# Gate and up products of an fp32 feed-forward layer: seven block products per pair of weight units in place of per unit

## What is computed

```python
D_MODEL, SEQ, D_FF = 1024, 256, 2816
x = rms_norm_2(h, g_pre_ffn)                  # 256 x 1024
gate, up = split(x @ w_gate_up, 2, axis=-1)   # w_gate_up: 1024 x 5632
y = (silu(gate) * up) @ w_down                # w_down: 2816 x 1024
h = h + rms_norm_2(y, g_post_ffn)
```

## Time and profile before

| | |
|---|---|
| median of three runs | 1509.06 us (1507.21 to 1509.69) |
| the profiled execution | 1509.1 us |
| its span, first to last instruction | 1507.3 us |
| mean granted TensorE clock | 0.948 |
| TensorE busy over the span | 1258.5 us (83%) |
| VectorE, ScalarE, GpSimd busy | 426.8, 283.0, 49.9 us |
| moved by DMA | 493.24 MB, mean 327 GB/s |

### The profile page before, as it was taken

One profiled execution on the slowest core, in us unless ns is written; L12 is line 12 of the kernel. 1 busy time (PEld: TensorE's weight loads), 2 busy tenths in 40 slices (PEclk: granted clock), 3 DMA queues, 4 the chain that ended last, 5 costly groups with the idle time before them and its releaser, 6 DMA issues.

```text
span 1507.3 us, 32779 instructions
## 1 busy us (share of the span) xinstructions
PE 1258.5 (83%) x14574; PEld 925.6 (61%) x14574; DVE 426.8 (28%) x862; ACT 283.0 (19%) x687; POOL 49.9 (3%) x90
## 2 busy tenths in 40 slices
PE   8999977678777778687776777777899999999998
PEld 5565855556555556565555565565555586888854
DVE  1653222122121121221221211212224213466644
ACT  3433212011121110210120111111212222211100
POOL 4101000000000000000000000000100000000000
PEclk9999999999899997998999899989999999999999
DMA  9529899999999999999999999999963342464420
GB/s 342 191 90 363 365 428 427 429 428 429 429 427 429 428 429 430 427 429 427 429 430 427 429 427 429 430 427 429 404 236 110 112 163 76 139 196 168 167 84 28
DMA packets 78597, 493.24 MB, mean 327 GB/s; under 512 B 4856, under 2 KB 28624, under 8 KB 53856
## 3 DMA queue, kind: packets, MB, share of 16 engines
q1 hardware_dynamic: 76560, 486.69, 78.8%
q0 software_dynamic: 1600, 5.17, 1.2%
q10 hardware_dynamic: 400, 0.86, 0.1%
HBM read 491.65 MB, written 1.05 MB: 327 GB/s over the span
## 4 chain that ended last, share of the span: by engine, by line
DMA 54%; PE 44%; issue 1%; DVE 1%; POOL 1%; SPq 0%; ACT 0%; DVEq 0%; POOLq 0%
DMA ring<-in_w_gate_dram 45%; PE bank L1345 7%; PE bank L1056 6%; PE bank L1157 6%; PE bank L690 5%; DMA ring<-in_w_down_dram 5%; PE bank L1380 4%; PE bank L777 3%; PE bank L714 2%; PE bank L1310 2%; DMA ring<-in_w_up_dram 2%; PE bank L1085 1%; PE bank L671 1%; DMA ring<-in_w_in_dram 1%; PE bank L1071 1%
## 5 line engine op out<-in xcount | busy, mean ns | idle before, releaser
L1056 PE MATMUL bank<-ring,big 128*32 128x128 f32 x8192 | 301.3, 309 | 179.7 <-DMA ring<-in_w_gate_dram 119.5
L1056 PEld LDWEIGHTS bank<-ring,big 128*32 128x32 f32 x8192 | 260.5, 124 | 230.2 <-DMA ring<-in_w_gate_dram 90.6
L1085 PE MATMUL bank<-ring,big 128*32 128x256 f32 x2048 | 130.2, 395 | 46.8 <-DMA ring<-in_w_down_dram 46.1
L2099 DVE TENSOR_TENSOR big<-big,bank 128x128 f32<-128x128 f32 x64 | 24.2, 378 | 470.6 <-PE bank L1056 470.6
L1600 ACT ACTIVATE big<-bank 32x256 f32<-32x256 f32 x128 | 47.9, 374 | 438.1 <-PE bank L1085 436.6
L1085 PEld LDWEIGHTS bank<-ring,big 128*32 128x32 f32 x2048 | 67.1, 112 | 86.2 <-issue 34.2
L2110 DVE COPY big<-bank 32x256 f32<-32x256 f32 x128 | 54.1, 423 | 226.8 <-PE bank L1085 224.9
L1157 PE MATMUL bank<-ring,xT 128*128 128x512 f32 x192 | 85.2, 594 | 0.3 <-ACT xT L1439 0.3
L690 PE MATMUL bank<-ring,xT 128*128 128x512 f32 x192 | 84.0, 593 | 0.0
L1071 PEld LDWEIGHTS bank<-aux,c 128*128 128x128 f32 x512 | 65.5, 201 | 15.0 <-issue 15.0
L1071 PE MATMUL bank<-aux,c 128*128 x512 | 74.3, 290 | 0.0
(11 more groups left out here) (373 smaller groups left out, 1408.2 us busy)
## 6 DMA issues: line engine op xcount, KB each, us to landing
ring<-in_w_gate_dram SPq DMA_DIRECT2D x64, 2048.0 KB, 25.8
ring<-in_w_up_dram SPq DMA_DIRECT2D x64, 2048.0 KB, 27.1
ring<-in_w_down_dram SPq DMA_DIRECT2D x63, 2048.0 KB, 27.1
ring<-in_w_gate_up_dram SPq DMA_DIRECT2D x22, 1024.0 KB, 7.0
ring<-in_w_in_dram SPq DMA_DIRECT2D x14, 1024.0 KB, 17.3
ring<-in_w_down_dram SPq DMA_DIRECT2D x12, 1024.0 KB, 6.9
ring<-in_w_in_dram SPq DMA_DIRECT2D x3, 2048.0 KB, 27.0
ring<-in_w_out_dram SPq DMA_DIRECT2D x2, 2048.0 KB, 18.3
```

Of the source, the lines that this page charges most:

```text
L1056: i = pe.matmul(dst[TOK * j:TOK * (j + 1), 0:P], xg[:, k, TOK * q:TOK * (q + 1)], w[:, k, j * P:(j + 1) * P], start=(k == 0), stop=(k == K ...
L1085: i = pe.matmul(bank[6 + q % 2][TOK * m:TOK * (m + 1), 0:SEQ], hT[:, q % 2, TOK * k:TOK * (k + 1)], w[:, k, SEQ * m:SEQ * (m + 1)], start= ...
```

## The change

`GU_FIRST` becomes 1: one plain unit, with two calls of `hidden` per token tile. The other ten units are taken as five pairs. The column halves of the block scheme are now the two units of a pair, so a block is 512 columns wide (256 gate, 256 up), a block product is four matmuls of 512 columns into a whole bank, and a weight sum covers 2048 elements a partition. There is one home for t1, t2 and t4 in place of two; the sums of the next pair's t1 and t2 wait for P5 of this pair, t4 for P4. TensorE's order becomes P1, P6, first turn of the pair before, P2, second turn, P5, P7, wait for ScalarE's copy of P7 (and for t4), P4, P3. The first slot of a pair is handed back after P4, the second after P3. A turn still has four transposes; each pair has two. The sums signal one by one (`gs_T`), and the buffers for P1, P7, P5 and the joined results exist once. The down products use other banks and homes, in the same order; the turns of the last pair come before P5 and before P7 of the first down unit.

```diff
-GU_FIRST = 2
-GU_SEVEN = N_GU - GU_FIRST
+GU_FIRST = 1
+GU_PAIRS = (N_GU - GU_FIRST) // 2
...
-                         *(("gu_mm", 2 * u + 2) if u < GU_FIRST else ("gs_mm", 7 * (u - GU_FIRST) + 7))))
+                         *(("gu_mm", 2 * u + 2) if u < GU_FIRST else ("gs_mm", 7 * ((u - GU_FIRST) // 2) + 6 + (u - GU_FIRST) % 2))))
...
         def gate_up_parts(i):
 
-            w = post_slot(12 + GU_FIRST + i).rearrange("p (j k w n c) -> p j k w n c", j=2, k=4, w=2, n=2)
-            return ([w[:, j, :, :, n, :] for j in range(2) for n in range(2)],
-                    [gs_T[i % 2][:, 1024 * m:1024 * (m + 1)].rearrange("p (k w c) -> p k w c", k=4, w=2) for m in range(3)])
+            w = [post_slot(12 + GU_FIRST + 2 * i + n).rearrange("p (j k c) -> p j k c", j=2, k=4) for n in range(2)]
+            return [w[n][:, j, :, :] for j in range(2) for n in range(2)], gs_T
 
         def gate_up_bank(i, m):
-            return bank[(4 * (i + 1) + m) % 7][:, 0:SEQ]
-
-        def gate_up_buffers(i):
-
-            b = (xn_flat[:, 0:1536], aux[:, 6144:7680])[i % 2]
-            return ([b[:, SEQ * m:SEQ * (m + 1)] for m in range(3)], b[:, 768:1536].rearrange("p (m w c) -> p m w c", m=3, w=2),
-                    xn_flat[:, 1536 + P * (i % 2):1536 + P * (i % 2 + 1)])
-
-        gs_T = [aux[:, 0:3072], aux[:, 3072:6144]]
+            return bank[(4 * (i + 1) + m) % 7][:, :]
+
+        gs_T = [aux[:, 2048 * m:2048 * (m + 1)].rearrange("p (k c) -> p k c", k=4) for m in range(3)]
+        gs_p1, gs_p7, gs_p5 = (xn_flat[:, 512 * m:512 * (m + 1)] for m in range(3))
+        gs_e11 = [xn_flat[:, 1536 + 256 * n:1536 + 256 * (n + 1)] for n in range(2)]
+        gs_quads = aux[:, 6144:7680].rearrange("p (m w c) -> p m w c", m=3, w=2)
...
-            for j in range(4):
+            for j in range(2 * GU_FIRST):
...
-            for j in range(4):
+            for j in range(2 * GU_FIRST):
                 hidden(j, P, SEQ)
+            def gate_up_turn(i, n):
+
+                rows = (gs_e11[i % 2], gs_quads[:, 1, 0, :]) if n == 0 else (gs_quads[:, 0, 0, :], gs_quads[:, 2, 0, :])
+                pe.wait_ge(*gs_at("gated", i))
+                pe.wait_ge(*at("ff_h", 2 * (GU_FIRST + 2 * i + n)))
+                for c in range(2):
+                    for t in range(TT):
+                        k = pe.transpose(bank[7][:, (2 * c + t) * P:(2 * c + t + 1) * P], rows[t][:, c * P:(c + 1) * P], ident)
                 k.then_inc(S("gs_tp"), 1)
...
                 def block_product(m, left, right, first):
                     for k in range(4):
-                        j = pe.matmul(gate_up_bank(i, m), left[:, k, :], right[:, k, :, :], start=(first and k == 0), stop=(k == 3),
+                        j = pe.matmul(gate_up_bank(i, m), left[:, k, :], right[:, k, :], start=(first and k == 0), stop=(k == 3),
                                       skip_group_check=not first)
                     j.then_inc(S("gs_mm"), 1)
 
-                post_wait(pe, 12 + GU_FIRST + i)
+                post_wait(pe, 12 + GU_FIRST + 2 * i)
                 if i >= 2:
                     pe.wait_ge(*gs_at("join", i - 2))
                 block_product(0, gs_x[0][0], b11, True)
-                pe.wait_ge(*gs_at("sums", i))
+                pe.wait_ge(*gs_at("t2", i))
                 block_product(1, s2, t2, True)
+                if i >= 1:
+                    gate_up_turn(i - 1, 0)
                 pe.wait_ge(*gs_at("p1", i))
                 block_product(0, gs_x[0][1], b21, False)
+                pe.wait_ge(*at("ff_h", 2 * GU_FIRST))
                 if i >= 1:
-                    gate_up_turn(i - 1)
+                    gate_up_turn(i - 1, 1)
+                block_product(3, s1, t1, True)
+                pe.wait_ge(*gs_at("b12", i))
                 block_product(2, s3, b12, True)
-                if i >= 1:
-                    pe.wait_ge(*gs_at("mult11", i - 1))
-                pe.wait_ge(*at("ff_h", 4))
-                block_product(3, s1, t1, True)
                 pe.wait_ge(*gs_at("p7", i))
+                pe.wait_ge(*gs_at("t4", i))
                 block_product(2, gs_x[1][1], t4, False)
-                pe.wait_ge(*gs_at("p5", i))
                 block_product(3, s4, b22, False)
...
-                        pe.wait_ge(*gs_at("join", GU_SEVEN - 2))
+                        pe.wait_ge(*gs_at("join", GU_PAIRS - 2))
                     if (n, name) == (0, "P5"):
-                        gate_up_turn(GU_SEVEN - 1)
+                        gate_up_turn(GU_PAIRS - 1, 0)
+                    if (n, name) == (0, "P7"):
+                        gate_up_turn(GU_PAIRS - 1, 1)
...
+            for i in range(GU_PAIRS):
                 if i >= 1:
                     gate_up_rest(i - 1)
                 act.wait_ge(*at("gs_mm", 7 * i + 1))
-                A(p1, gate_up_bank(i, 0), ACT.Copy).then_inc(S("gs_act"), 1)
+                A(gs_p1, gate_up_bank(i, 0), ACT.Copy).then_inc(S("gs_act"), 1)
+                if i >= 1:
+                    gate_up_turned(i - 1, 0)
                 act.wait_ge(*at("gs_mm", 7 * i + 3))
                 if i >= 2:
-                    act.wait_ge(*at("gs_tp", i - 1))
-                A(e11, gate_up_bank(i, 0)[:, 0:P], ACT.Silu).then_inc(S("gs_act"), 1)
+                    act.wait_ge(*at("gs_tp", 2 * i - 3))
+                A(gs_e11[i % 2], gate_up_bank(i, 0)[:, 0:256], ACT.Silu).then_inc(S("gs_act"), 1)
+                if i >= 1:
+                    gate_up_turned(i - 1, 1)
                 act.wait_ge(*at("gs_mm", 7 * i + 4))
-                A(p7, gate_up_bank(i, 2), ACT.Copy).then_inc(S("gs_act"), 1)
-                if i >= 1:
-                    gate_up_turned(i - 1)
+                A(gs_p5, gate_up_bank(i, 3), ACT.Copy).then_inc(S("gs_act"), 1)
                 act.wait_ge(*at("gs_mm", 7 * i + 5))
-                A(p5, gate_up_bank(i, 3), ACT.Copy).then_inc(S("gs_act"), 1)
-            gate_up_rest(GU_SEVEN - 1)
-            gate_up_turned(GU_SEVEN - 1)
+                A(gs_p7, gate_up_bank(i, 2), ACT.Copy).then_inc(S("gs_act"), 1)
...
                 if part == 0:
-                    post_wait(dve, 12 + GU_FIRST + i)
-                    if i >= 2:
-                        dve.wait_ge(*at("gs_mm", 7 * i - 7))
-                    link(V.tensor_tensor(t1, b12, b11, ALU.subtract))
+                    for n in range(2):
+                        post_wait(dve, 12 + GU_FIRST + 2 * i + n)
+                    if i >= 1:
+                        dve.wait_ge(*at("gs_mm", 7 * (i - 1) + 4))
+                    V.tensor_tensor(t1, b12, b11, ALU.subtract).then_inc(S("gs_T"), 1)
+                    dve.wait_ge(*gs_at("t1", i))
                 elif part == 1:
-                    link(V.tensor_tensor(t2, b22, t1, ALU.subtract))
+                    V.tensor_tensor(t2, b22, t1, ALU.subtract).then_inc(S("gs_T"), 1)
+                    dve.wait_ge(*gs_at("t2", i))
                 elif part == 2:
-                    V.tensor_tensor(b12, b22, b12, ALU.subtract)
+                    V.tensor_tensor(b12, b22, b12, ALU.subtract).then_inc(S("gs_T"), 1)
                 else:
-                    V.tensor_tensor(t4, b21, t2, ALU.subtract).then_inc(S("gs_dve"), 1)
+                    if i >= 1:
+                        dve.wait_ge(*at("gs_mm", 7 * (i - 1) + 6))
+                    V.tensor_tensor(t4, b21, t2, ALU.subtract).then_inc(S("gs_T"), 1)
...
+                if i >= 1:
+                    gate_up_gate(i - 1)
+                dve.wait_ge(*at("gs_mm", 7 * i + 2))
+                dve.wait_ge(*gs_at("p1", i))
+                link(V.tensor_tensor(gs_p1, gs_p1, gate_up_bank(i, 1), ALU.add))
+                if i >= 1:
+                    down_rows(i - 1)
+                dve.wait_ge(*gs_at("silu11", i))
+                V.tensor_tensor(e11, e11, gate_up_bank(i, 0)[:, 256:512], ALU.mult).then_inc(S("gs_dve"), 1)
                 if more:
                     gate_up_sums(i + 1, 0)
+                    gate_up_sums(i + 1, 1)
+                else:
+                    down_sums(0)
+                dve.wait_ge(*gs_at("p7", i))
+                link(V.tensor_tensor(gs_p7, gs_p7, gs_p1, ALU.add))
                 if i >= 1:
-                    gate_up_gate(i - 1)
-                if more:
-                    gate_up_sums(i + 1, 1)
-                dve.wait_ge(*at("gs_mm", 7 * i + 2))
-                dve.wait_ge(*gs_at("p1", i))
-                link(V.tensor_tensor(p1, p1, gate_up_bank(i, 1), ALU.add))
+                    dve.wait_ge(*at("gs_tp", 2 * i))
+                V.tensor_tensor(c22, gs_p7, gs_p5, ALU.add)
                 if more:
                     gate_up_sums(i + 1, 2)
                     gate_up_sums(i + 1, 3)
-                else:
-                    down_sums(0)
-                dve.wait_ge(*gs_at("silu11", i))
-                V.tensor_tensor(e11, e11, gate_up_bank(i, 0)[:, P:2 * P], ALU.mult).then_inc(S("gs_dve"), 1)
-                dve.wait_ge(*gs_at("p7", i))
```

(58 more changed lines are left out.)

5 lines of the change are left out of this document (3 added, 2 removed).

## The result

The changed kernel takes 1513.41 us (median of 10 runs, 1511.43 to 1515.79) against 1508.68 for the kernel before (10 runs, 1506.94 to 1512.46): ratio 1.0029, 95% interval 1.0019 to 1.0039, so slower by some 0.3%. The profiled execution took 1513.1 us, its span is 1511.3, mean granted clock 0.943.

The account below looks back on a forecast made before the run. TensorE's gapless stream after 1291.87 was taken to bound the end one for one. -2.51 + 1.52 + 4.90 = +3.91 us on 1509.06 gave 1513.0 us (+0.26%), range 1508.0 to 1516.0.

Parts of the forecast that it names:

- The work itself: TensorE's plain and block products: one plain unit dropped, wider blocks, one turn more; net -2.51 us.
- The width's 0.7: Block products: doubling the width alone saves 0.7 us over 35 products.
- The start loses cover: Before the second tile's plain products: TensorE waits for ScalarE's copy of that tile, +1.52 us (1.34 to 1.7).
- A wait without cover in every pair: Between P7 and P4: ScalarE's copy of P7 is uncovered, 0.98 us in five pairs, +4.9 us (4.0 to 5.5).
- After the pairs: Down products begin at about 1437.2 instead of 1433.83; after that TensorE's stream is as long as now.
- What stays hidden: Inside the pairs: sums, "gated", turns and unit loads come in time, 9.9 us spare for next sums; no wait.
- The clock: Stretch of pairs: granted clock stays 1.00, no term; rival has it at 0.91, +11.9 us, 1524.9 us, chance 0.04.
- the P7 wait costs nothing: Rival, between fifth and sixth product: the bank's copy is covered, sum -1.0, 1508.1 us; chance 0.15.
- the single home costs time: Rival, at P6: next pair's t1 and t2 come only after "gated", 4.0 us four times, 1529 us; chance 0.03.
- the wide product's cost: Rival, block products: a wide one isn't twice the narrow; at 3.35 each, -2.9 us more, 1510.1 us; chance 0.02.

Follow-up runs that it names:

- the new order in the kernel before: Kernel before (256 columns, two homes, two plain units) with only P5 issued ahead of P7: 1514.72 us, ratio 1.0042.
- the two narrow matmuls: Changed kernel with every 512-column block matmul issued as two of 256 columns, weights loaded for each: one run, 1517.79 us, stretch 210.46 us.
- the turn in the gap: Changed kernel with the second turn of four transposes moved from before P5 to between P7 and P4: one profiled run, stretch 207.99 us.

## Why the prediction was right

1513.0 us was forecast and 1513.41 measured; the stretch was to grow by 3.91 us and grew by 3.81. That the time came within 0.4 us is in part luck: the forecast started from 1509.06, ten runs beside the changed kernel gave 1508.68, and from there it would have said 1512.6. The stretch is the better witness. Step by step:

- *The work itself, -2.51.* With both waits removed the stretch is 2.47 under that of before. The width's 0.7 was measured by itself as 0.69. Right.
- *The start loses cover, +1.52.* Issuing P1 early took 1.51 off. Right. The forecast 1301.62 had the slower first load in it; measured are 1301.69 and 0.10 for that load, less the 0.19 by which the whole stretch is later: 1301.60.
- *A wait without cover in every pair, +4.90.* Measured 0.95 rather than 0.98 a pair, 4.78 by the run that took it away. The mechanism is right, the term 0.12 too large: I charged 0.08 between the copy and the weight load, from a place where VectorE's copy ended last; after ScalarE's copy it is 0.04.
- *After the pairs.* The down products were to begin at about 1437.2 and began at 1437.39, 0.19 of it from ahead. But the stream behind that was not "as long as now": 64.44 us to the last piece in place of 64.00, since the added turn lies in the first down unit. The sum counts that turn once, with the work of the pairs, so it stands; only the place was wrong.
- *What stays hidden.* No wait on VectorE or on a transfer. 2048 elements take 2.29 us, as extended from shorter rows; "gated" ends 2.75 into the second pair (1335.72 + 0.96 - 1333.93), forecast 2.8. The single home was no matter even 3.4 us later.
- *The clock.* The granted clock stayed 1.00, with idles of 0.69 us in 26 and also with those of 1.18 where the copy was doubled. This is that kernel's row, again with the columns of the earlier trace rows; the clock is the 1.00 near its end. The Trainium skill (page "TensorE: Matmul & The Clock Gate", section "A second HAM failure mode: psum-queue depth-cycling") reports for a bf16 kernel that short idles between groups of matmuls make the clock oscillate. These fp32 runs do not show it: the clock is 1.00 in every stretch above.

```profile
1320.00:1440.00 120.00, 114.12 (x288) 51.05 (x287) 68.89 (x68) 21.23 (x36) 0.00 (x0) 1.00 0.44 151
```

- *Rivals.* That the P7 wait costs nothing is refuted by five idles; that the single home costs time, by the run with P7 first and by the new order in the kernel before; the wide product's cost by the rows at 3.43.

What is not settled: the medians differ by 4.73 us and the stretches by 3.81. The interval of the ratio, +2.9 to +5.9 us, holds both, so the runs do not show that the rest needs a cause.

## What to carry to other kernels

When two products share a bank and the first must be copied out before the second may start, the products between them are what hides the copy; changing their order (here P5 went first, whose sum t1 is there before P7's b12) puts copy and hand-off on the path, once per round. Widening a matmul from 256 to 512 columns saved almost nothing here (a product took 3.454 us in two halves and 3.433 whole), so judge such a change by the waits that it makes and by the work that it drops. Work that is dropped may have been cover: look for what lay beside it, and move up something that needs only the inputs already there.

## What the runs showed of the hardware

The stretch does not begin at the same time in each execution: between 1290.48 and 1296.06 us in eleven profiles, although all edits lie behind that point. That is more than the 3.81 us of the change, while the stretch itself gave the same length to 0.01 us (203.49 and 203.50 in two executions of one kernel). For an edit behind such a start, the stretch tells from one profile what the total needs many runs for.

The spread is older than the expert loop. From the start of the loop's last piece to the start of the stretch all eleven took 215.29 or 215.30 us, and the loop itself, from its first product to that piece, 919.1 to 919.9. But its first product started anywhere from 155.84 to 160.98, and that goes with TensorE's granted clock. In the four latest (159.2 and more) the clock was 0.94 from 30 to 60 us and 0.96 or 0.97 from 100 to 155; in the four next (157.5 to 157.7) 1.00 and 0.97; in the three earliest (up to 156.3) 1.00 in both. Here are the latest, with the two narrow matmuls, and the earliest but one, with the turn in the gap; columns as in the earlier trace rows.

```profile
30.00:60.00 30.00, 28.69 (x88) 17.07 (x89) 12.65 (x15) 13.92 (x25) 6.57 (x4) 0.94 0.80 290
100.00:155.00 55.00, 54.03 (x271) 34.51 (x271) 21.35 (x59) 17.68 (x35) 7.90 (x14) 0.96 0.71 265
...
30.00:60.00 30.00, 29.93 (x100) 17.48 (x101) 13.88 (x19) 14.51 (x26) 5.33 (x4) 1.00 0.88 326
100.00:155.00 55.00, 53.75 (x280) 34.28 (x279) 22.93 (x74) 18.62 (x39) 8.53 (x16) 1.00 0.76 286
```

The profiles of the kernel before and of the changed one are both of the middle group, with first products of the loop at 157.48 and 157.54, so their difference has next to nothing of this. What makes the clock fall in some executions is not settled.

The first piece after a wait takes 0.10 us longer (3.70 in place of 3.60), at 256 columns as at 512; in one place, after a wait for VectorE, it was 0.08.
